# Half-size products of the dense layers, each issued as two products of 64 output columns

## The reference

```python
def conv_ffn(x, w_up, conv_w, conv_b, w_down):
    hid = causal_dwconv(x @ w_up, conv_w, conv_b)
    gate, val = jnp.split(hid, 2, axis=-1)
    return (jax.nn.gelu(gate) * val) @ w_down
```

```python
def swiglu(h, w_gate, w_up, w_down):
    return (jax.nn.silu(h @ w_gate) * (h @ w_up)) @ w_down
```

## Time and profile before

| what | value |
|---|---|
| median of 3 runs | 2281.91 us |
| lowest, highest run | 2281.67 us, 2285.21 us |
| span of the profiled execution | 2281.3 us |
| mean granted TensorE clock | 0.989 |
| PE (matmul) busy | 2211.3 us, 97% |
| PEld (weight load) busy | 2019.5 us, 89% |
| VectorE (DVE) busy | 871.5 us, 38% |
| ScalarE (ACT) busy | 467.1 us, 20% |
| moved by DMA | 522.45 MB, mean 229 GB/s |

### The profile page before, as it was taken

One profiled execution on the slowest core, in us unless ns is written; L12 is line 12 of the kernel. 1 busy time (PEld: TensorE's weight loads), 2 busy tenths in 40 slices (PEclk: granted clock), 3 DMA queues, 4 the chain that ended last, 5 costly groups with the idle time before them and its releaser, 6 DMA issues.

```text
span 2281.3 us, 67869 instructions
## 1 busy us (share of the span) xinstructions
PE 2211.3 (97%) x30612; PEld 2019.5 (89%) x30612; DVE 871.5 (38%) x2198; ACT 467.1 (20%) x1074; POOL 3.3 (0%) x10
## 2 busy tenths in 40 slices
PE   9999999999999999999978999999999999999998
PEld 8879998857899876999966899999999999999998
DVE  4257765224766536567678210101010101111101
ACT  3432112123211234110043211111111111111111
POOL 0000000000000000000000000000000000000000
PEclk9999999999999999999999999999999999999999
DMA  7142444232144322444322199999999999999996
GB/s 322 74 166 96 155 159 164 92 129 111 70 160 160 134 81 105 190 158 158 119 98 93 56 337 398 330 399 343 393 339 391 353 368 374 359 381 344 390 355 253
DMA packets 103298, 522.45 MB, mean 229 GB/s; under 512 B 8402, under 2 KB 8531, under 8 KB 95443
## 3 DMA queue, kind: packets, MB, share of 16 engines
q1 hardware_dynamic: 103122, 519.82, 59.3%
HBM read 518.74 MB, written 1.05 MB: 228 GB/s over the span
## 4 chain that ended last, share of the span: by engine, by line
PE 61%; DVE 3%; ACT 1%; issue 1%; DVEq 0%; ACTq 0%
PE ps L1731 26%; PE ps L1745 13%; PE ps L1126 6%; PE ps L1159 4%; PE ps L1056 3%; PE ps L1521 2%; PE ps L1718 1%; PE ps L1689 1%; DVE scr L2393 1%; PE ps L1703 0%; PE ps L1391 0%; PE ps L1377 0%; PE ps L1458 0%; PE ps L1504 0%; PE ps L1353 0%
## 5 line engine op out<-in xcount | busy, mean ns | idle before, releaser
L1731 PE MATMUL ps<-scr,slot 128*64 128x96 f32 x14336 | 636.6, 246 | 2.8 <-issue 2.7
L1731 PEld LDWEIGHTS ps<-scr,slot 128*64 128x64 f32 x14336 | 610.9, 137 | 4.0 <-issue 3.7
L1745 PE MATMUL ps<-scr,slot 128*64 128x96 f32 x7168 | 341.3, 247 | 0.0
L1745 PEld LDWEIGHTS ps<-scr,slot 128*64 128x64 f32 x7168 | 313.3, 137 | 24.0 <-issue 24.0
L2522 DVE TENSOR_TENSOR scr<-scr,ps 128x96 f32<-128x96 f32 x224 | 56.5, 252 | 611.8 <-PE ps L1731 611.8
L1159 PE MATMUL ps<-scr,slot 128*128 128x256 f32 x1056 | 244.7, 387 | 7.9 <-DVE scr L2210 7.9
L1159 PEld LDWEIGHTS ps<-scr,slot 128*128 128x128 f32 x1056 | 200.3, 195 | 34.9 <-DVE scr L2210 9.5
L908 ACT ACTIVATE scr<-ps 128x96 f32<-128x96 f32 x224 | 56.1, 250 | 824.9 <-PE ps L1731 824.9
L1126 PE MATMUL ps<-vtok,slot 128*128 128x128 f32 x1056 | 139.8, 276 | 2.7 <-DVE vtok L2150 2.7
L1126 PEld LDWEIGHTS ps<-vtok,slot 128*128 128x128 f32 x1056 | 128.6, 192 | 3.5 <-DVE vtok L2150 3.5
L1126 PE MATMUL ps<-vtok,proj 128*128 128x128 f32 x1056 | 128.7, 275 | 0.0
(11 more groups left out here) (391 smaller groups left out, 2127.3 us busy)
## 6 DMA issues: line engine op xcount, KB each, us to landing
slot<-in_w_moe SPq DMA_DIRECT2D x224, 1024.0 KB, 7.1
slot<-in_w_moe SPq DMA_DIRECT2D x224, 512.0 KB, 6.9
slot<-in_w_ffn SPq DMA_DIRECT2D x33, 3072.0 KB, 10.2
slot<-in_w_even_in SPq DMA_DIRECT2D x3, 3072.0 KB, 27.4
slot<-in_w_odd_qk SPq DMA_DIRECT2D x2, 3072.0 KB, 10.9
slot<-in_w_s_glu SPq DMA_DIRECT2D x2, 3072.0 KB, 11.3
slot<-in_w_odd_v SPq DMA_DIRECT2D x2, 2048.0 KB, 8.2
slot<-in_w_even_in SPq DMA_DIRECT2D x2, 1536.0 KB, 11.8
```

The costliest lines, as they stand in the source:

```text
L1731: m = pe.matmul(pair(f, k)[s:s + STRIP, 0:CAP], w[:, o:o + STRIP], xg[e % 2][:, c], start=c == 0, stop=c == KD - 1, skip_group_check=True)
L1745: m = pe.matmul(y_sum(d)[s:s + STRIP], w[:, o:o + STRIP], hid[f % 4][:, 0:CAP], start=f == 0 and d % 5 == 0, stop=f == FE_TILES - 1, skip_ ...
```

## The change

In `dense_seven` on TensorE both places that issue the half-size products now issue each matmul twice, over 64 columns of the weights each, into the partitions 0 to 63 and 64 to 127 of the same region. Operands, order, waits and the semaphore of the last matmul stay.

```diff
                 def four(k, n, weights, x, first):
 
                     for c in range(4):
-                        m = pe.matmul(product(k, n), weights[:, c * P:(c + 1) * P], x[:, c],
-                                      start=first and c == 0, stop=c == 3, skip_group_check=True)
+                        for s in range(0, P, STRIP):
+                            m = pe.matmul(product(k, n)[s:s + STRIP],
+                                          weights[:, c * P + s:c * P + s + STRIP], x[:, c],
+                                          start=first and c == 0, stop=c == 3, skip_group_check=True)
                     return m
...
                     for k in range(2):
                         w = w_block(phase, 0, k, c // 4, 0)
-                        pe.matmul(product(k, (P1, P2)[c // 4]), w[:, c % 4 * P:c % 4 * P + P],
-                                  x_half[0][c // 4][:, c % 4], start=c == 0, stop=c % 4 == 3,
-                                  skip_group_check=True)
+                        for s in range(0, P, STRIP):
+                            o = c % 4 * P + s
+                            pe.matmul(product(k, (P1, P2)[c // 4])[s:s + STRIP], w[:, o:o + STRIP],
+                                      x_half[0][c // 4][:, c % 4], start=c == 0, stop=c % 4 == 3,
+                                      skip_group_check=True)
```

## The result

| | before | changed |
|---|---|---|
| median (6 runs each) | 2281.79 us | 2292.59 us |
| lowest, highest | 2280.51, 2289.54 us | 2288.27, 2293.97 us |
| span of the profiled execution | 2281.3 us | 2290.7 us |

The change makes the kernel slower by about 0.4%: ratio 1.0041, 95% interval 1.0029 to 1.0054 (the ratio is not the quotient of the two medians, which is 1.0047). The forecast was 2293.4 us, with a range of 2288.5 to 2298.5. In a second set, of 12 runs against 23, the ratio was 1.0042 (1.0026 to 1.0058).

What follows compares the result with a forecast made beforehand. The prediction took TensorE (PE) to bound the dense stages: 58 pairs of turns between whole and half form cost 20.2 us, halves save 8.7 us, so 2281.9 + 11.5 = 2293.4 us, range 2288.5 to 2298.5.

Steps and rivals of the forecast that it cites:

- The bound: Dense stages: PE is the bound, busy 97% of the span, so its added time reaches the end one for one.
- The gain, 2.4 ns per record: Half-size products of the dense stages: halves lose the 2.4 ns surplus over the stream on 3632 records, -8.7 us.
- The rival that the 2.4 ns stay: Half-size products: no gain from halves, only the turns count, 2302.1 us; chance 6%.
- The turns, 0.348 us a pair: Dense stages: PE going to the whole form and back costs 0.348 us a pair, 20.2 us for 58 pairs.
- Its split: Within one pair of turns: 0.10 us wait after the last half, 0.05 first record, 0.10 late finish, 0.10 before the first half.
- The bounds of 0.28 and 0.41: Lower and upper limit in us for the price of one pair of turns, giving 2289.4 and 2297.0 us.
- The prediction's estimate of 0.33 a pair: Price of a pair of turns from the skill's 398-cycle constant as one drain: 0.17 us a turn, sum 1 us smaller.
- The number of turns, 58 pairs: Dense stages: 19 pairs per stage between halves and down(), 57 in all, plus one at the start of ffn2.
- The last turn of ffn0 and ffn1: Stage ends: the last turn to the whole form hides in PE's 3.15 us wait for the hidden tile, costing nothing.
- The sum: Whole kernel: 20.2 us for turns less 8.7 us gain, +11.5 us on 2281.9 us.
- only moved: Stages other than the dense ones, the expert stage included: they only move in time, at no cost.
- the rival of one slow stretch gone: Ends of ffn0 and ffn1: one half-clock stretch after the 3.15 us pauses disappears, 2290.2 us; chance 7%.

Runs made afterwards that it cites:

- experts_whole: Kernel before, with the expert stage's products made whole at 128 columns instead of halves: 2580.48 us (two runs), ratio 1.1314 to the kernel before.
- down_in_halves_only: Kernel before, with down() alone in halves and the half-size products left whole: 2298.14 us, ratio 1.0081 to the kernel before.
- turns_doubled: Changed kernel, with one of the five summed products (P7) left whole between halves: 2313.09 us, ratio 1.0142 to the kernel before.

## Why the prediction was right

*The bound.* PE was and stayed the bound of the dense stages; its round grew by what the turns cost and nothing took up the slack. Right.

*The gain, 2.4 ns per record.* Right and now isolated: 6.11 us for 28 products without turns, against 6.25, or 2.5 ns per record. The prediction took the 2.4 ns from rows and gave no reason for them. experts_whole shows that they are not the stream's (111.6 ns at 96 columns), and the transposes with their shorter loads (109 ns) point to the weight load. The rival that the 2.4 ns stay would have had a round of 10.06 us; it was 9.92, and 9.57 without turns, so that rival is out. The Trainium skill (TensorE: Matmul & The Clock Gate, LDWEIGHTS) gives a load as columns / 1.2, 107 ns for 128 columns. The trace disagrees if that is the pace of a stream of float32 records: 111.6 ns a record at 96 columns and 112 at 8.

*The turns, 0.348 us a pair.* The round gives 9.92 - 9.71 + 0.14 = 0.35, down_in_halves_only 0.34, turns_doubled 0.35. Its split was right as well. By the starts of the records of the changed kernel (medians over the turns of the dense stages) the first whole record starts 0.202 us after the last half where 0.103 is the pace, and the next one 0.320 after it where 0.216 is; the first half starts 0.309 us after the last whole record (0.216), and the next pair 0.160 after it (0.109). The surplus is 0.10 + 0.10 on the way to the whole form and 0.09 + 0.05 on the way back, 0.35 together. The bounds of 0.28 and 0.41 were not needed. The Trainium skill (TensorEngine Tiling (Array Packing), Key Properties) says that a change of tiling mode drains the TensorE. The trace agrees: in both directions the first load of the new form starts 0.07 us before the recorded end of the last record of the old form, where the first load of down() started 0.11 us ahead of its first matmul before the change. The prediction's estimate of 0.33 a pair, from the latency formula of the Trainium skill (TensorE: Matmul & The Clock Gate, Single matmul latency), is 0.02 us under the measured 0.35; that the drain is that constant is not shown.

*The number of turns, 58 pairs.* Right: 58 late loads in both directions. The last turn of ffn0 and ffn1 is hidden, as the pauses of 2.97 and 2.96 instead of 3.15 us show.

*The sum.* +11.5 us in the dense stages, measured +11.5 in the mean of the profiles and 11.2 with the clock alike. In whole runs it was 10.8 in the first set and 9.0 in the second. The difference is not in the named steps. About 2.8 us came on in the expert stage, which the prediction had as "only moved"; that step failed, and its cause is open. It was given back in the rest of the program (2.1 us in the profiles) and, by the medians, a little beyond that. So that the whole comes within 0.8 us of the forecast is in part luck: terms that the sum did not have cancel. Part of the scatter is the clock, which the prediction had as the rival of one slow stretch gone, with 7%. It put that too low: the two profiles of before differ by 4.4 us in ffn0 and ffn1 with nothing changed.

## What to carry to other kernels

Splitting a product into two halves of 64 columns pays where its whole form takes longer than its stream, so in float32 below some 130 streaming columns (an estimate from the 111.6 ns: 2 x 131 / 2.4 + 2.5 = 111.7), and by the difference. A turn to the whole form costs 0.20 us and one to the halves 0.14, so halves pay only over long runs: here a run of 28 products saves 0.14 us and a pair of turns costs 0.35, and putting the neighbour into the same form, though it wins nothing itself, turned +9 us into -6 (medians against the kernel before on the same chip). Count the turns first, then the records.

## What was not expected of the hardware

The same 32 records behind the same pause of 3.15 us took 10.02 us in one execution of the kernel before and 7.17 in another, by whether the clock fell to 1.2 GHz behind the pause. The two profiles of that kernel differ by 5.8 us in their spans (2281.3 and 2275.5), so a smaller difference between two kernels cannot be read from the spans of single profiles; the rounds repeat to 0.01 us. The pace of a whole float32 record is the same, near 111.6 ns, at 8, 96 and 128 streaming columns. And the pauses of the expert stage, in which PE waits for nothing that the profile shows, recur behind the same records from one execution to the next.
